# A hybrid convolution and linear-attention layer on eight cores: the context tile shares its first FFN's weight blocks with the fourth token tile, first loads in another order, one stream order for all sequences

## The chip, the cores and the metric

The kernel runs on all eight cores of one Trainium2 chip. The batch of 32 sequences is split over the cores, four to a core; the cores exchange nothing. The metric is the device time of the slowest core, in microseconds. The kernel before took 7987.3 us (median of three runs, 7969.67 to 7999.19).

## The reference, cut to what matters

```
x: (32, 2048, 1024) tokens    ctx: (32, 256, 1024) context tokens    D_FF = 2816
mx = split(silu(c) @ w_mod + b_mod, 9)          # shift, scale, gate for ffn1, mixer, ffn2
mc = split(silu(c_ctx) @ w_mod + b_mod, 9)      # the same map, for context tokens
half_ffn(h, ...): u = rmsnorm(h) * (1 + scale) + shift
                  a, b = split(u @ w_gu); h + 0.5 * gate * ((silu(a) * b) @ w_down)
x = half_ffn(x, ..., w1_gu, w1_down);  h = half_ffn(ctx, ..., w1_gu, w1_down)
# one input projection: conv input | q | k | v | output gate | decays | merge gates
# of the context only k, v and the decays are used: they give the start state of both scans
o = forward scan + backward scan (chunked gated linear attention, 4 heads)
y_conv = silu(layernorm(depthwise_conv31(glu(conv_in)))) @ w_conv_out
y_gla  = (rmsnorm(o) * silu(og)) @ w_gla_out
x = x + gate * ((sigmoid(ga) * y_conv + sigmoid(gb) * y_gla) @ w_out)
x = half_ffn(x, ..., w2_gu, w2_down);  out = rmsnorm(x) * g_final
```

## The kernel before

Activations lie with channels on partitions: a token tile is 8 x 128 channels by 512 tokens, and a sequence has four of them (i = 0 to 3) and a context tile of 256 tokens (i = 4). `JOBS` lists, for each sequence s, five "A" jobs (first FFN of tiles 0 to 3, then of the context) and four "D" jobs (second FFN of tiles 0, 3, 1, 2). `GID` numbers them; g is that number, nine to a sequence.

The program is made of streams, each a Python generator that yields groups of instructions. A scheduler (`Sched.run`) merges them into one fixed order for each engine: it holds a modelled time for each engine, each tile and the DMA, takes first a group without matmuls that could start within 1.5 us of TensorE's modelled time, else the first stream in order of priority whose matmul group is ready, else the group that is ready soonest. Streams wait for flags that other streams set; a flag only orders the instructions, while the semaphores that the program waits on come from the tiles that an instruction reads and writes. Each engine works through its own list in order; SP issues most DMAs, and GpSimd (POOL) issues the casting ones (fp32 to bf16) among its additions and powers.

The streams that matter here:

- `mod_stream` (priority 9): 36 half-chunks of w_mod, 1 MB each, into two buffers `WM` (in the trace wm_82 and wm_83); the first eight give shift and scale of the first FFN (flag ("mod", 1)), the others are spread over the FFN steps by `MOD_AT`.
- `n_stream` (8): `n1(job)` loads x in 128-token pieces into xtok, transposes it on TensorE into `X[g % 2]`, normalises and modulates it into `uF[g % 2]`; `n2(job)`, after the FFN, stores X (2 MB, x1_s) for a token tile and modulates into `U2[i]` for the mixer. n1 of the next tile goes before n2 of the present one.
- `f_stream` (3, raised to 5 for the first D job of sequence 0): for each job 22 up-projection steps (one 512 KB block `wgu`, 16 matmuls, silu on ACT, product on DVE) into hF, then 8 down-projection steps (one 704 KB block `wdn`, 22 matmuls). Flags ("fs", 30 g + step) mark the steps. Jobs 0 and 1 of sequence 0 already share their up-projection blocks (`pair`, second hidden tile hF2). `WL` fetches blocks ahead: where a weight is used for the first time it is cast by a POOL DMA and written back to a bf16 copy in HBM by SP, later it is loaded from that copy by SP.
- `pc_stream`, `pz_stream`, `pq_stream`, gate and state streams: the mixing stage. The convolution's projections start with tiles 0 and 1; q, k, v with tile 0 of head 0; both scans start from the context tile.
- `mp_stream`, `mh_stream`, `m_stream` (4.5, 4.6, 4): LayerNorm and head norms of each tile, then the merge, whose result feeds the D job of the tile. X alternates between two buffers, so the merge of one tile waits for the output of the D job two before its own (flag ("p", g - 2)).
- `c_stream` (1): in sequence 0 it casts 70 weights (48 of 256 KB in bf16, two buffers, and 22 of 512 KB, one buffer) for later stages, one for each mark; its marks are ("fs", 88) to ("fs", 149) and eight convolution steps. `setup` holds the first loads.

The lines the trace names: L638 is the DMA helper, L649 the matmul helper, L653 transposes, L665 ACT, L674 tensor_tensor, L677 scalar_tensor_tensor.

## Time and profile before

| | us |
|---|---|
| median of three runs | 7987.3 |
| the profiled execution | 7996.9 |
| its span on the slowest core | 7995.3 |
| TensorE busy in it | 7500.6 |
| VectorE, ScalarE, GpSimd busy | 2871.8, 2794.9, 1378.8 |

The page divides the span into 40 slices of some 200 us. TensorE's digit is 6 in the first slice, 9 in nearly all others, with 7 and 8 in some. All numbers of rows come from core 1, the slowest one. A matmul's recorded duration runs to the end of its pipeline, so a row's mean is longer than the step from one matmul to the next. In sequence 0 the first FFN runs from about 95 to 737 us, the mixing to about 1258, merge and second FFN to 2213; sequence 1 has its context stage from 2695 to 2766 us.

### The profile page before, as it was taken

The numbers are of one execution on the slowest core, as the hardware profiler recorded it, in microseconds if no ns is written. First come the engines' busy times: TensorE is split into PE (matmuls) and PEld (weight loads), VectorE is DVE, ScalarE is ACT, GpSimd is POOL, SyncE is SP. The second block draws the span as 40 slices with busy tenths as digits, with TensorE's granted clock in tenths as the row PEclk, the third lists the DMA queues.
The fourth block names the chain that finished last, engine by engine and source line by source line (L and its number), as shares of the span: only waits on it lengthen the run. The fifth ranks groups of instructions, "written<-read, shape, count | busy, mean of one in ns | idle before, by whom it ended". The sixth has DMA issues, their size and how long they took to land.

```text
span 7995.3 us, 125533 instructions; the slowest of 8 cores (7951.7 to 7995.3 us)
## 1 busy us (share of the span) xinstructions
PE 7500.6 (94%) x43682; PEld 3886.1 (49%) x43682; DVE 2871.8 (36%) x4652; ACT 2794.9 (35%) x5010; POOL 1378.8 (17%) x1138
## 2 busy tenths in 40 slices
PE   6997989789999999899999999999999999989999
PEld 3444544344444555444444464544444455544444
DVE  1221555222232256433232234633322324653322
ACT  2222664222222266422122245632222325653221
POOL 0111114222001100422101000141211011033210
PEclk8999999899999999999999998999999999999999
DMA  7888775364555524545555543554555562354544
GB/s 193 232 259 211 170 180 152 127 186 160 166 182 184 181 79 119 158 153 168 164 179 183 184 128 86 135 165 165 172 160 170 186 200 85 93 167 148 176 160 143
DMA packets 489205, 1300.37 MB, mean 163 GB/s; under 512 B 56464, under 2 KB 156048, under 8 KB 477840
## 3 DMA queue, kind: packets, MB, share of 16 engines
q1 hardware_dynamic: 468720, 1236.57, 49.1%
q0 software_dynamic: 19872, 55.78, 4.6%
q8 instruction: 367, 6.01, 0.3%
q14 instruction: 246, 2.02, 0.1%
HBM read 1166.36 MB, written 181.53 MB: 169 GB/s over the span
## 4 chain that ended last, share of the span: by engine, by line
PE 80%; DMA 10%; issue 3%; ACT 2%; DVE 2%; POOL 1%; SPq 1%; DVEq 0%; ACTq 0%; POOLq 0%
PE pb L649 78%; PE pb L653 2%; SPq L638 1%; DMA xtok_85<-x 1%; DMA L0rz_135<-z_s 1%; DMA wgu_96<-gu_s 1%; DMA wdn_101<-dn_s 1%; DMA wgu_95<-gu_s 0%; DMA L1rz_193<-z_s 0%; DMA wf_s<-w2k_80 0%; DMA w2k_80<-w_in_f 0%; POOL mac_118 L674 0%; DMA wgu_97<-gu_s 0%; DMA xtok_84<-x 0%; DMA w2k_81<-wf_s 0%
## 5 line engine op out<-in xcount | busy, mean ns | idle before, releaser
L674 DVE TENSOR_TENSOR hF<-ft_102,pb 128x512 bf16<-128x512 f32 (+1 forms) x396 | 260.2, 657 | 855.6 <-PE pb L649 739.8
L674 DVE TENSOR_TENSOR hF<-ft_103,pb 128x512 bf16<-128x512 f32 (+1 forms) x374 | 244.9, 655 | 748.4 <-PE pb L649 684.8
L665 ACT ACTIVATE ft_103<-pb 128x512 f32<-128x512 f32 (+1 forms) x396 | 225.6, 570 | 736.1 <-PE pb L649 732.2
L665 ACT ACTIVATE ft_102<-pb 128x512 f32<-128x512 f32 (+1 forms) x396 | 225.5, 569 | 730.0 <-PE pb L649 725.3
L649 PE MATMUL pb<-hF,wdn_100 128*128 128x512 bf16 (+1 forms) x2068 | 448.8, 373 | 15.8 <-DMA wdn_100<-dn_s 11.5
L649 PE MATMUL pb<-hF,wdn_101 128*128 128x512 bf16 (+1 forms) x2046 | 432.2, 367 | 10.7 <-DMA wdn_101<-dn_s 7.1
L649 PE MATMUL pb<-hF,wdn_99 128*128 128x512 bf16 (+1 forms) x2046 | 430.9, 366 | 11.7 <-DMA wdn_99<-dn_s 6.4
L649 PE MATMUL pb<-uF_88,wgu_97 128*128 128x512 bf16 (+1 forms) x1712 | 378.7, 374 | 25.3 <-ACT ft_102 L665 18.0
L649 PE MATMUL pb<-uF_89,wgu_95 128*128 128x512 bf16 (+1 forms) x1728 | 378.7, 371 | 8.8 <-ACT ft_102 L665 5.9
L677 DVE SCALAR_TENSOR_TENSOR X_86<-pb,SC,X_86 128x512 f32<-128x512 f32 (+1 forms) x208 | 151.9, 730 | 638.2 <-PE pb L649 633.1
L649 PE MATMUL pb<-uF_89,wgu_96 128*128 128x512 bf16 (+1 forms) x1728 | 374.6, 368 | 5.1 <-DMA wgu_96<-gu_s 5.1
L649 PE MATMUL pb<-uF_88,wgu_98 128*128 128x512 bf16 (+1 forms) x1712 | 372.1, 369 | 1.5 <-DMA wgu_98<-gu_s 1.4
L677 DVE SCALAR_TENSOR_TENSOR X_87<-pb,SC,X_87 128x512 f32<-128x512 f32 (+1 forms) x208 | 151.9, 730 | 609.6 <-PE pb L649 609.4
L649 PE MATMUL pb<-uF_89,wgu_98 128*128 128x512 bf16 (+1 forms) x1440 | 317.7, 373 | 13.3 <-ACT ft_103 L665 11.8
L649 PE MATMUL pb<-uF_88,wgu_96 128*128 128x512 bf16 (+1 forms) x1456 | 319.1, 370 | 11.8 <-ACT ft_103 L665 5.9
L649 PE MATMUL pb<-uF_88,wgu_95 128*128 128x512 bf16 (+1 forms) x1456 | 318.0, 370 | 10.3 <-DMA wgu_95<-gu_s 10.3
L649 PE MATMUL pb<-uF_89,wgu_97 128*128 128x512 bf16 (+1 forms) x1440 | 315.5, 370 | 10.5 <-DMA wgu_97<-gu_s 10.5
L649 PEld LDWEIGHTS pb<-hF,wdn_100 128*128 128x128 bf16 x2068 | 202.8, 98 | 247.7 <-issue 28.0
L649 PEld LDWEIGHTS pb<-hF,wdn_99 128*128 128x128 bf16 x2046 | 200.1, 98 | 228.5 <-issue 17.0
L649 PEld LDWEIGHTS pb<-hF,wdn_101 128*128 128x128 bf16 x2046 | 200.6, 98 | 226.8 <-issue 15.7
L649 PEld LDWEIGHTS pb<-uF_88,wgu_97 128*128 128x128 bf16 x1712 | 169.9, 100 | 210.8 <-issue 39.1
L649 PEld LDWEIGHTS pb<-uF_89,wgu_95 128*128 128x128 bf16 x1728 | 170.0, 99 | 194.5 <-issue 19.2
(730 smaller groups left out, 13378.0 us busy)
## 6 DMA issues: line engine op xcount, KB each, us to landing
wgu_97<-gu_s SPq DMA_DIRECT2D x187, 512.0 KB, 4.0
wgu_98<-gu_s SPq DMA_DIRECT2D x187, 512.0 KB, 4.1
wgu_95<-gu_s SPq DMA_DIRECT2D x187, 512.0 KB, 4.1
wgu_96<-gu_s SPq DMA_DIRECT2D x187, 512.0 KB, 4.1
wdn_101<-dn_s SPq DMA_DIRECT2D x91, 704.0 KB, 4.7
wdn_99<-dn_s SPq DMA_DIRECT2D x91, 704.0 KB, 4.6
wdn_100<-dn_s SPq DMA_DIRECT2D x90, 704.0 KB, 4.7
w2k_78<-wf_s SPq DMA_DIRECT2D x166, 256.0 KB, 3.1
```

The lines of the kernel that those rows point to most:

```text
L638: S.op(q, lambda e: e.dma_start(out=out, in_=in_, **kw), reads, writes, float(nb), dma=True)
L649: S.op("pe", lambda e: e.matmul(out, lhsT, rhs, start=start, stop=stop), reads, writes, c)
L653: S.op("pe", lambda e: e.transpose(out, in_, idn), reads, writes, c)
L665: S.op("act", lambda e: e.activation(out, in_, func, **kw), reads, writes, c)
L674: S.op(eng, lambda e: e.tensor_tensor(out, in0, in1, op), reads, writes, vcost(eng, fsz(out), fast))
L677: S.op("dve", lambda e: e.scalar_tensor_tensor(out=out, in0=in0, scalar=scalar, in1=in1, op0=op0, op1=op1), reads, writes, vcost("dve", fs ...
```

## The change

The context's first FFN no longer has steps of its own. In tile 3's job each weight block is used first for the context (256 columns), then for tile 3 (512 columns), in the up- and in the down-projection. For that the context has its own X (`Xc`, in the bytes of the merge buffers MTM), modulated input (`uFc`, in MRB) and hidden tile (`hF2c`, in the bytes of U2_3 and half of U2_4); its n1 follows n1 of tile 3, both before n2 of tile 2, and its n2 follows n2 of tile 3. Flags of both jobs are set at the end of the shared steps.

The first loads: wal, dwp, rmask, smask and gfin move from `setup` to `setup_later`, after step 4; w_mod has three buffers for its first eight half-chunks; the first weight blocks are asked for after half-chunk 5 (flag "mw"); tile 0 does its first three steps alone before tile 1 is waited for.

The order: the raised priority of `f_stream` in sequence 0 is gone; the blocks of all jobs of a sequence are listed at once; `c_stream` may issue two casts for each step of tile 3's job and one at each of the first eight convolution steps. `pc_stream` asks for its first blocks at step 8 of tile 3's job.

```diff
+              sb("wm2", [128, 4, 512], F32, Area([(loc_lo[0], loc_lo[1])]))]
+        hF2c, t_hF2c = sb("hF2c", [128, NJ, 256], BF16, Area([(loc_lo[3], loc_lo[3] + 12288)]), parts=NJ)
+        Xc = sb("Xc", [128, 8, 256], F32, Area([span_of(rts(MTM))]), parts=8)
+        uFc = sb("uFc", [128, 8, 256], BF16, Area([span_of(rts(MRB))]), parts=8)
...
+        def setup_later():
+            dma("sp", wal[:], wal_d, writes=[t_wal], nb=256 * 1024)
...
+            dma("sp", gfin[:], gfin_d[0:1, :].to_broadcast((128, D)), writes=[t_gfin], nb=512 * 1024)
...
+            wbuf = lambda cc: WM[cc % 3 if cc < 8 else cc % 2]
...
+                S.flag(("mw", cc))
...
+                if cc + 3 < 8:
+                    fetch(cc + 3)
...
+        def XB(job):
+            return Xc if job[1] == "A" and job[2] == 4 else X[GID[job] % 2]
...
-                if nxt < len(JOBS) and JOBS[nxt][1] == "A":
+                if nxt < len(JOBS) and JOBS[nxt][1] == "A" and JOBS[nxt][2] < 4:
...
                     yield from n1(JOBS[nxt])
+                    if JOBS[nxt][2] == 3:
+                        yield from n1(JOBS[nxt + 1])
...
-                    if s == 0:
-                        S.prio("f", 5)
...
+                if kind == "A" and i == 4:
+                    continue
...
+                if g == 0:
+                    yield ("wait", ("mw", 5))
...
+                two = kind == "A" and i == 3
+                jobs = [JOBS[1], job] if g == 0 else [JOBS[g + 1], job] if two else [job]
+                if g == 1:
+                    steps = []
+                elif g == 0:
+                    steps = [(0, [1]), (1, [1]), (2, [1]), (0, [0]), (1, [0]), (2, [0])] + [(j, [0, 1]) for j in range(3, NJ)]
+                else:
+                    steps = [(j, list(range(len(jobs)))) for j in range(NJ)]
...
+                for k, (j, which) in enumerate(steps):
...
+                    for x in which:
+                        jb = jobs[x]
+                        if g == 0 and k in (3, 6):
+                            yield ("wait", ("u", 1))
+                        if two and j == 0:
+                            yield ("wait", ("u", g + 1))
...
+                    for jb in (jobs if two else [job]):
+                        Xb, tX = XB(jb)
...
                 S.flag(("f", g))
-                if s == 0 and kind == "D" and i == 0:
-                    S.prio("f", 3)
+                if two:
+                    S.flag(("fs", 30 * (g + 1) + 29))
+                    S.flag(("f", g + 1))
...
-                b = LB[GID[(s, "A", 4)] % 2]
+                b = LB[GID[(s, "A", 3)] % 2]
...
-                yield ("wait", ("u", g))
+                yield ("wait", ("fs", 30 * (g - 1) + 8))
...
-            marks = [("fs", 88 + k) for k in range(62)] + [("cv", 0, c, i) for c in range(2) for i in range(4)]
+            fs = [("fs", 88), ("fs", 89)] + [("fs", 90 + k // 2) for k in range(60)]
+            marks = fs + [("cv", 0, c, 0) for c in range(8)]
+            yield ("wait", ("fs", 4))
+            setup_later()
```

## Rows read from the trace of the kernel before

**Rows 1.** The page's busy time of each engine (share, count)

```profile
PE 7500.6 (94%) x43682; PEld 3886.1 (49%) x43682; DVE 2871.8 (36%) x4652; ACT 2794.9 (35%) x5010; POOL 1378.8 (17%) x1138
```

**Rows 2.** By stretch: length, engines' busy us (count), clock, DMA share, GB/s

```profile
0.00:103.10 103.10, 38.29 (x362) 28.95 (x363) 18.39 (x36) 27.83 (x48) 5.69 (x12) 0.75 0.72 190
510.50:640.40 129.90, 122.04 (x565) 56.40 (x564) 31.31 (x50) 30.75 (x54) 22.53 (x31) 0.97 0.93 247
640.40:737.00 96.60, 68.50 (x546) 55.52 (x545) 19.13 (x39) 17.80 (x39) 14.15 (x22) 0.89 0.92 254
2577.50:2695.30 117.80, 117.80 (x565) 55.85 (x564) 31.49 (x50) 30.64 (x54) 10.56 (x9) 1.00 0.58 188
2695.30:2766.50 71.20, 63.18 (x545) 54.09 (x544) 18.98 (x39) 17.82 (x39) 6.63 (x8) 0.95 0.73 245
```

**Rows 3.** The same, sum over context stages of sequences 1, 2, 3

```profile
sum 215.20, PE 189.26 PEld 161.87 DVE 56.94 ACT 53.49 POOL 19.88; mean PE 63.09 PEld 53.96 DVE 18.98 ACT 17.83 POOL 6.63
```

**Rows 4.** Matmuls of sequence 1's context stage: busy us, mean ns, idle

```profile
L649 PE MATMUL pb<-hF,wdn_99 128*128 128x256 bf16 x66 | 7.7, 272 | 1.8 <-DMA wdn_99<-dn_s 1.6
```

**Rows 5.** TensorE's waits in that stage: us in total, times, longest

```profile
PE pb L649 <- DMA wgu_97<-gu_s: 4.5, 1, 4.5
```

**Rows 6.** DMA issues in that stage: count, KB each, median us to landing

```profile
x_s<-X_86 SPq DMA_DIRECT2D x1, 2048.0 KB, 11.1
```

**Rows 7.** Busy by stretch: merge and second FFN, sequences 0 and 1; a part

```profile
1375.00:2213.20 838.20, 763.38 (x3609) 372.40 (x3610) 237.26 (x346) 196.17 (x324) 169.20 (x135) 0.95 0.51 159
3363.40:4129.70 766.30, 746.30 (x3599) 361.84 (x3598) 236.37 (x346) 194.89 (x323) 162.93 (x127) 0.98 0.51 166
1530.00:1630.00 100.00, 46.96 (x184) 30.89 (x183) 32.68 (x47) 26.87 (x43) 35.89 (x28) 0.65 0.27 74
```

**Rows 8.** TensorE's waits in the first of these: us, times, longest

```profile
PE pb L649 <- POOL mac_117 L674: 22.0, 1, 22.0
```

**Rows 9.** Tile and context U: ns min/median/max, first and last start

```profile
L665 ACT ACTIVATE U_3_67<-ntm_109,SC x4: 712/722/722, 2706.7 to 2711.8; 128x512 bf16<-128x512 f32 x4
...
L649 PE MATMUL pb<-U_4_68,wq_70 x16: 272/273/283, 2804.5 to 2831.8; 128*128 128x256 bf16 x16
L665 ACT ACTIVATE U_4_68<-ntm_109,SC x4: 492/501/508, 2780.3 to 2788.5; 128x256 bf16<-128x256 f32 x4
```

**Rows 10.** DMA from 2 to 28 us: queues' share of 16 engines; an issue

```profile
q0 software_dynamic: 720, 2.43, 66.2%
q1 hardware_dynamic: 1268, 2.31, 32.4%
...
xtok_84<-x SPq DMA_DIRECT2D x1, 512.0 KB, 23.1
```

**Rows 11.** DMA from 32.3 to 73 us: the same two

```profile
q1 hardware_dynamic: 1558, 9.86, 75.1%
...
xtok_84<-x SPq DMA_DIRECT2D x1, 512.0 KB, 8.0
```

**Rows 12.** Timeline of the start: start us, duration us, instruction

```profile
32.33 0.42 SPq L638 DMA_DIRECT2D wm_82<-w_mod  x1
...
75.84 0.23 DVE L677 SCALAR_TENSOR_TENSOR SC<-modT,vecs 128x40 f32<-128x40 f32 x1
...
95.43 3.62 PE L649 MATMUL pb<-uF_88,wgu_95 128*128 128x512 bf16 x16
```

**Rows 13.** Casts of sequence 0, first and last of 33; bytes of that stretch

```profile
515.31 0.57 POOL L638 DMA_DIRECT2D w2k_80<-w_in_f  x1 [1.56 <-DMA wf_s<-w2k_80]
...
736.41 0.57 POOL L638 DMA_DIRECT2D w2k_80<-w_conv_out  x1
...
DMA packets 18855, 56.65 MB, mean 250 GB/s; under 512 B 2096, under 2 KB 2096, under 8 KB 18455
```

**Rows 14.** Cold w2_down in sequence 0: ns, first and last start

```profile
L649 PE MATMUL pb<-hF,wdn_100 x43: 379/379/631, 1630.1 to 1649.8; 128*128 128x512 bf16 x43
L638 POOL DMA_DIRECT2D wdn_100<-w_down x2: 532/586/639, 1605.7 to 1636.7; - x2
```

More of the change, by code:

```diff
@@ L770, in mod_stream @@
                 if cc == 0:
-                    fetch(0)
-                    fetch(1)
+                    for k in range(3):
+                        fetch(k)
                 elif MOD_AT[cc] > 0:
@@ L851, in modulate, with UB @@
                 yield
+        def XB(job):
+            return Xc if job[1] == "A" and job[2] == 4 else X[GID[job] % 2]
+        def UB(job):
+            return uFc if job[1] == "A" and job[2] == 4 else uF[GID[job] % 2]
         t_x1 = [T(f"x1_{i}") for i in range(NTT)]
@@ L919, in n2 @@
             W, col = jw(job), jcol(job)
-            Xb, tX = X[g % 2]
+            Xb, tX = XB(job)
             acc, t_acc = accF[g % 2]
@@ L972, in n_stream @@
                     yield from n1(job)
-                if job[1] == "D" and job[2] == 0:
-                    pass
-                if nxt < len(JOBS) and JOBS[nxt][1] == "A":
+                if nxt < len(JOBS) and JOBS[nxt][1] == "A" and JOBS[nxt][2] < 4:
                     if g >= 1:
@@ L1013, in f_stream @@
                 yield ("wait", ("u", g))
-                Xb, tX = X[g % 2]
-                u, tu = uF[g % 2]
-                gn = 2 if kind == "A" else 8
-                acc, t_acc = accF[g % 2]
-                sides = [(u, tu, hF, t_hF)]
-                if pair:
-                    yield ("wait", ("u", 1))
-                    sides.append((uF[1][0], uF[1][1], hF2, t_hF2))
-                hb_, t_hb = (hF2, t_hF2) if g == 1 else (hF, t_hF)
-                for j in (() if g == 1 else range(NJ)):
-                    wb, t_wb = wl_g.get(ng)
-                    ng += 1
-                    S.flag(("fs", 30 * g + j))
-                    for (uu, tuu, hh_, t_hh) in sides:
+                two = kind == "A" and i == 3
[6 more added lines that the diff above has]
+                    steps = [(j, list(range(len(jobs)))) for j in range(NJ)]
+                hid = {job: (hF2, t_hF2) if g == 1 else (hF, t_hF)}
+                if len(jobs) == 2:
+                    hid[jobs[0]] = (hF2, t_hF2) if g == 0 else (hF2c, t_hF2c)
+                wj = {}
+                for k, (j, which) in enumerate(steps):
+                    if j not in wj:
+                        if g == 0 and j < 3:
+                            wl_g.ahead = 3 - j
+                        wj[j] = wl_g.get(ng)
+                        wl_g.ahead = 3
+                        ng += 1
+                        S.flag(("fs", 30 * g + j))
+                    wb, t_wb = wj[j]
+                    for x in which:
[4 more added lines that the diff above has]
+                            yield ("wait", ("u", g + 1))
+                        uu, tuu = UB(jb)
+                        hh_, t_hh = hid[jb]
+                        W = jw(jb)
                         pa, t_pa = FB.next()
@@ L1040, in f_stream @@
                         yield
-                if s == 0 and kind == "A" and i == 0:
+                if g == 0:
                     yield ("wait", ("mod", 2))
+                gn = 2 if kind == "A" else 8
                 for o in range(8):
@@ L1055, in f_stream @@
-                    yield
-                    if o == 0:
-                        act(acc[:, :W], Xb[:, o, :W], AF.Square, [tX[o]], [t_acc])
+                    for jb in (jobs if two else [job]):
+                        Xb, tX = XB(jb)
+                        acc, t_acc = accF[GID[jb] % 2]
+                        W, col = jw(jb), jcol(jb)
+                        hb_, t_hb = hid[jb]
+                        pd, t_pd = FB.next()
+                        for j in range(11):
+                            mm(pd[:, :W], wb[:, j, :], hb_[:, j, :W], j == 0, False, [t_wb, t_hb[j]], [t_pd])
@@ L1058, in f_stream @@
                         yield
-                    else:
-                        sq, t_sq = FQ.next()
-                        act(sq[:, :W], Xb[:, o, :W], AF.Square, [tX[o]], [t_sq])
+                        for j in range(11, NJ):
+                            mm(pd[:, :W], wb[:, j, :], hb_[:, j, :W], False, j == NJ - 1, [t_wb, t_hb[j]], [t_pd])
                         yield
-                        tt(acc[:, :W], acc[:, :W], sq[:, :W], ALU.add, [t_acc, t_sq], [t_acc], eng="pool")
+                        stt(Xb[:, o, :W], pd[:, :W], SC[:, col, gn, o:o + 1], Xb[:, o, :W], ALU.mult, ALU.add, [t_pd, t_SC[gn], tX[o]], [tX[o]])
@@ L1064, in f_stream @@
                         yield
+                        if o == 0:
+                            act(acc[:, :W], Xb[:, o, :W], AF.Square, [tX[o]], [t_acc])
+                            yield
+                        else:
+                            sq, t_sq = FQ.next()
+                            act(sq[:, :W], Xb[:, o, :W], AF.Square, [tX[o]], [t_sq])
+                            yield
+                            tt(acc[:, :W], acc[:, :W], sq[:, :W], ALU.add, [t_acc, t_sq], [t_acc], eng="pool")
+                            yield
```

69 lines of the change are left out of this document (28 added, 41 removed).

## The prediction

> **What bounds the kernel now.** I began with the busy shares: TensorE is busy for 94% of the span [rows 1], so only the stretches where it is not can give anything. Then I cut the span at the stage borders and read each stretch against one that does the same work undisturbed [rows 2]. An FFN tile of 512 tokens in sequence 1 takes 117.8 us with TensorE busy for all of it: there is nothing to gain there. The context tile that follows takes 71.2 us, and in sequences 1 to 3 together it takes 215.2 us [rows 3]. Its matmuls have 256 columns. One group of 66 is busy 7.7 us with 272 ns for one [rows 4]; it is three runs of 22, so one run is 2.57 us = 21 steps + 0.27, a step of 0.109 us. Its 22 x 16 + 8 x 22 = 528 matmuls need 57.6 us, plus some 1.9 us for the 17 others in the stretch (545 in all [rows 2]): 59.5 us, 178.5 for three. What is above that, 36.7 us, goes with the wait for weights: the longest one is for wgu_97 [rows 5], and beside it stands the 2 MB store of the tile before, 11.1 us to landing [rows 6]. Half the columns use up the same weight bytes in half the time. In sequence 0 the same two stages take 129.9 + 96.6 = 226.5 us against 117.8 + 59.5 = 177.3.
>
> Two more stretches stand out. The first 103.1 us have 38.3 us of matmul [rows 2]. And the merge with the second FFN of sequence 0 takes 838.2 us, where sequence 1 takes 766.3 for the same work [rows 7]: 71.9 us more. In it lies a stretch of 100 us with TensorE busy 47.0 at a granted clock of 0.65 [rows 7]; the longest wait there is 22.0 us for a GpSimd addition of the LayerNorm [rows 8]. In the other sequences the up-projection fills these gaps; here it ran before them, in one piece, under its raised priority.
>
> **The change part by part.** The terms are made against the profiled execution, 7996.9 us (span 7995.3 and 1.6 around it), which is 0.12% above the median of the three runs, 7987.3.
>
> Context tile with token tile 3, sequences 1 to 3. Each block of 16 matmuls a side is now used for 16 x 0.109 + 16 x 0.22 = 5.3 us (0.22 is 117.8 us by 528) where the context stage used it for 1.7, and the reload of 22 x 512 and 8 x 704 KB, 16.9 MB, goes in each sequence. The loads of a 512-column tile are hidden at 3.5 us a block [rows 2], so they are at 5.3. I take 1 us a sequence as left: +33.7. What is moved: the context's n1 goes into tile 2's FFN, where ACT and DVE are busy 31 us of 118 [rows 2], cost 0. The normalisations n2 of tile 3 and of the context now both come after the FFN, with the 2 MB store in front of them on SP's queue, and the first mixing loads behind it. Before, tile 3's last U step began 16.5 us after its FFN's end (2711.8 against 2695.3), and the context's eight took from about 2779 to 2789 and were first read at 2804.5, 38 us after the FFN's end at 2766.5 [rows 9]. In a row the two end after some 17 + 10 = 27 us, before the 38, so they are covered by the projections of tiles 0 to 2; if that cover were gone it would be 10 us a sequence. The store costs between 0 and its 11.1 us [rows 6] a sequence, because the convolution's own store and reload chain queues behind it; I take 3, nearer to 0 as the projections of tiles 0 to 2 need no new block at once. Term: 33.7 - 9 = **+25**, bounds +1 and +37.
>
> First loads. Before, x is asked for with the four casting weight loads of GpSimd and the broadcast of gfin in flight, and lands after 23.1 us [rows 10]; the first w_mod load waits in SP's order behind the reuse of that buffer and goes out at 32.33 [rows 12]. After the change only scT, vecs and cst are ahead of x, and the casts follow GpSimd's first pow, so x should land after about 8 us (this is what xtok took among the w_mod loads [rows 11]) and the first w_mod load go out at about 13: 19 us earlier. From there the modulation is ready 43.5 us later (32.33 to 75.84 [rows 12]). The casts now fall into that stretch: they took 66.2% of the engines for 26 us, 17 us of work [rows 10], while w_mod took 75.1% of 40.7 us, 30.6 us [rows 11]. The sum is 48 us at full use; the third buffer lets the gaps be used, so I take 50 us, 7 more than now. The modulation is ready 12 us earlier. Beside that, three column steps of tile 0 come before tile 1 is needed, where one did before (3.62 us [rows 12]): 7 us. Term: **+19**, bounds 0 (casts wholly in the way, 19 - 17, and the fillers hidden anyway) and +39 (no cast in the way).
> What the rows show of sharing is q0 at 66.2% and q1 at 32.4% while both had work [rows 10]. The Trainium skill (DMA: Bandwidth & Descriptors, Queues, rings and completion order) says that each engine goes round robin between queues, packet by packet. The trace agrees only in that both move; by an even turn x would have landed sooner in the kernel before, and the sum would lose some 5 us of the 19.
>
> Sequence 0, tile 3 with context. The excess there is 226.5 - 177.3 = 49.2 us. The conversion stream (fp32 to bf16 weights for later stages, a cast on GpSimd and a write-back on SP, two buffers) issued 33 casts from 515.31 to 736.41 [rows 13], 6.7 us each. Now two may be issued per block; the order on SP is fixed, so a write-back that waits for its cast holds the weight loads behind it. With 33 casts in the paired stage and 30% fewer bytes (16.9 of 56.65 MB [rows 13]) I expect about 5.3 us each, 175 us, so TensorE's 177 would bound; with 44 casts 233 us would. I take 211 us: **+15**, bounds -20 and +45. What is not cast there is cast in the mixing stage, so little is given back later.
> By the Trainium skill (DMA: Bandwidth & Descriptors, Anatomy of one DMA) a load costs about 2 us and its bytes at 436 GB/s; a cast and its write-back would take about 6 us for each buffer, 3 us for each of two, and this term would be +45. The rows show more than twice that for a cast, so I hold to them.
>
> One order in sequence 0. The second FFN loses its raised priority, so its up-projection no longer runs in one piece (before the norm and head work of the next tile) but fills that work's gaps, as in sequence 1. This takes away the 71.9 us, but not the cold w2_down: its first cast is issued at 1605.70 and the first matmul on it runs at 1630.1 [rows 14], 24.4 us. In the new order the next merge waits for that tile's output, so nothing covers these. Term: 71.9 - 24.4 = **+47**, bounds 0 and 72.
>
> Sum: 25 + 19 + 15 + 47 = 106 us. 7996.9 - 106 = 7891; scaled by 7987.3 / 7996.9 it is **7881 us**.
>
> **The rivals.** (a) The conversion stream throttles the paired stage. At 6.7 us for each of 60 casts it would last 402 us, 175 more than 226.5: 25 + 19 - 175 + 47 = -84, a time of 8071, slower than before. It decides from about 47 casts in that stage (47 x 6.7 = 315, which eats the other 91 us). For it: casts waited for write-backs in every step before. Against: only 33 went out where 60 were allowed, so the buffers set the pace and not the marks. (b) The order of sequence 0 gives nothing because the cold w2_down is put off until all else is done, as before: 47 of the gain are lost, 7928. (c) The mixing stages start later: store and two n2 exposed for 10 us in all four sequences, 40 of the gain are lost, 7921. The 11 us between 27 and 38 speak against it. (d) All goes well: casts out of the way (20 more), conversions hidden (30 more), the order worth all 72 (25 more): a gain of 181 instead of 106, 7806. (e) The edit does less than it says, the context's matmuls being bound by something other than weights (weight loading into the array, say): then 34 of the gain are lost, 7915; the 0.109 us step in rows that wait for nothing speaks against it.
>
> **How the numbers follow.** Forecast 0.58 (own range 7835 to 7925), (a) 0.05, (b) 0.13, (c) 0.10, (d) 0.10, (e) 0.04. The range reaches half-way to (d) and beyond (b), (c) and (e) by the forecast's own 20 us: 7810 to 7945. A measurement of this kernel can tell about 0.5%, 40 us, from no change: faster means under 7947, slower over 8027. The forecast and (d) are faster, most of (b), (c) and (e) too (0.20 of 0.27), with 0.07 in between; (a) is slower for 0.04 and in between for 0.01. So 0.88, 0.08, 0.04.
>
> **What would show it.** Right: paired stages of 175 to 180 us in sequences 1 to 3 (now 117.8 + 71.2 = 189) with no wait for wgu; the first w_mod load before 16 us and the first FFN matmul before 70; in sequence 0 a paired stage between 180 and 230 us; its merge stage at 780 to 800 us with no 22 us wait for mac_117. Wrong: a first read of the context's U later after the FFN's end than the 38 us of now, w_mod loads behind casts, or a paired stage in sequence 0 in which each block takes two cast round trips.

## The result, and the profile after

The changed kernel takes 7890 us (7887.1 and 7892.7), the kernel before 7987.3 at the median: a ratio of 0.988, 95% interval 0.9836 to 0.9925. That is some 97 us less, more than the 40 us that can be told from no change. The forecast was 7881, its range 7810 to 7945. Cores of a die whose granted clock lay under 0.96 are left out of all times in this document.

The time is that of the slowest core, and this is not the same core in the two profiles (core 1 before, core 6 after; within one run the cores lie up to 51 us apart). So I cut every core's trace at the same marks and took the mean over the eight cores, whose spans fell from 7974.7 to 7862.0 us, by 112.7. The marks: F, the last w1_down matmul of tile 2's FFN; E, the last one of the FFN of tile 3 and context; M, the first merge matmul on MT; N, the first product hF of the next sequence, or the end. In us, before, after and gained:

| stretch | sequence 0 | sequence 1 | sequence 2 | sequence 3 |
|---|---|---|---|---|
| start (or N) to F: tiles 0 to 2 | 508.3, 500.2: **8.1** | 361.8, 365.3: -3.5 | 361.5, 364.7: -3.2 | 362.0, 365.8: -3.8 |
| F to E: tile 3 and context | 230.9, 181.6: **49.3** | 188.7, 173.3: 15.4 | 189.3, 173.3: 16.0 | 189.8, 173.3: 16.5 |
| E to M: mixing | 604.0, 626.6: **-22.6** | 566.0, 573.9: -7.9 | 572.2, 574.9: -2.7 | 565.6, 575.9: -10.3 |
| M to N: merge and second FFN | 874.0, 808.6: **65.4** | 797.6, 798.6: -1.0 | 797.2, 800.2: -3.0 | 806.0, 805.8: 0.2 |

By the prediction's terms: first loads **8** (19 were forecast); sequence 0's tile 3 with context 49, of which 23 are given back in the mixing behind it, **27** (15); one order in sequence 0 **65** (47); tile 3 with context in sequences 1 to 3 47.9 - 10.5 - 20.9 - 3.8 = **13** (25). They add up to 113 where 106 stood: two terms that came out too small (by 23 us) stood against two that came out too large (by 30), so it is partly luck that the total was this near.

The same stretches on the page's core, by windows (length, engines' busy us and count, clock, DMA share, GB/s): the start, tile 3 with context in sequence 0, tile 2's FFN of sequence 1, tile 3 with context there, and sequence 0 from M to N.

```profile
0.00:72.00 72.00, 30.87 (x314) 22.71 (x316) 10.27 (x24) 16.86 (x29) 4.05 (x10) 0.71 0.78 213
497.74:678.09 180.35, 175.05 (x1056) 106.12 (x1073) 39.81 (x69) 35.37 (x69) 34.66 (x52) 0.99 0.84 207
2376.00:2499.16 123.16, 122.33 (x593) 60.47 (x604) 39.47 (x63) 42.59 (x75) 11.56 (x10) 1.00 0.58 192
2499.16:2672.62 173.46, 172.51 (x1056) 105.29 (x1073) 39.77 (x69) 35.38 (x69) 14.98 (x15) 1.00 0.32 110
1323.80:2135.10 811.30, 775.57 (x3681) 378.45 (x3754) 250.09 (x366) 206.77 (x343) 182.24 (x147) 0.98 0.54 167
```

The paired FFN of sequence 1 is TensorE from end to end at the full clock; its DMA share is 0.32, where the two stages had 0.58 and 0.73 [rows 2], and TensorE's waits in it show none for weights. All eight cores take 173.3 us for it in each of the three sequences. In sequence 0 it has 7 us more. The busy shares hardly move [rows 1], since what was removed was mostly idle time. The page's core lacks 733 of TensorE's 43682 records; on core 5, where none is missing before or after, TensorE's busy time fell by 25 us (7491.1 to 7466.1) and the span by 118 (7987.1 to 7868.7). The page:

```profile
PE 7426.2 (94%) x42949; PEld 3872.2 (49%) x43682; DVE 2885.0 (37%) x4652; ACT 2796.4 (35%) x5014; POOL 1379.5 (17%) x1138
```

TensorE's longest waits from 1388 to 2135 us (us in total, times, longest), for [rows 8]: the 22 us for mac_117 are gone, and the cold w2_down shows as 4.1 us.

```profile
PE pb L653 <- ACT ft_104 L669: 11.9, 2, 5.9
PE pb L653 <- DMA w2k_81<-wf_s: 6.7, 2, 6.3
PE pb L653 <- DMA wdn_102<-w_down: 2.7, 1, 2.7
...
PE pb L653 <- DMA wdn_103<-w_down: 0.8, 1, 0.8
PE pb L653 <- DMA wdn_101<-w_down: 0.6, 1, 0.6
```

Two places where time came back. The context's U in sequence 1 (ns min/median/max, first and last start; FFN's end at 2672.6), for [rows 9]: the last writes of tile 3's U start 24 us after the FFN's end, those of the context's 42, and its first read is at 2717.3, 45 us behind. Each tile's rows stand under its own view.

```profile
L669 ACT ACTIVATE U_3_67<-ntm_110,SC x4: 706/712/722, 2685.9 to 2695.6; 128x512 bf16<-128x512 f32 x4
L669 ACT ACTIVATE U_3_67<-ntm_111,SC x4: 705/710/721, 2686.5 to 2696.7; 128x512 bf16<-128x512 f32 x4
```

```profile
L653 PE MATMUL pb<-U_4_68,wq_70 x16: 272/273/283, 2717.3 to 2745.9; 128*128 128x256 bf16 x16
...
L669 ACT ACTIVATE U_4_68<-ntm_111,SC x4: 492/508/508, 2706.0 to 2714.6; 128x256 bf16<-128x256 f32 x4
```

And sequence 0 behind its paired FFN (timeline of TensorE: start, length, instruction, idle before it and its releaser). The broadcasts of the two norms (out of stn_58 and stn_59) stand in TensorE's queue ahead of the first head projection on U_0. U_0 was ready long before; the projection's weight wq_69 was asked for at 681.74 us and took 6.5 us to land, so about 7 of the 10 us of waiting fall after both were there:

```profile
681.94 1.02 PE L653 MATMUL pb<-ones_45,accF_109 128*128 128x1 f32 x8 [0.40 <-POOL accF_109 L678]
685.09 1.73 PE L653 MATMUL pb<-cst,stn_58 128*128 128x128 f32 x8 [2.12 <-POOL stn_58 L678]
686.61 0.85 PE L653 MATMUL pb<-ones_45,accF_108 128*128 128x1 f32 x4
695.37 1.19 PE L653 MATMUL pb<-cst,stn_59 128*128 128x128 f32 x4 [7.91 <-POOL stn_59 L678]
```

### The profile page after: what moved, and what is told of

It reads as the page before. It is cut to its first block, busy times and chain, and to the rows that moved or that the text cites. A ratio compares the mean times of both kernels' runs of the same rounds, so it can differ in the third digit from the quotient of the medians.

```text
span 7891.2 us, 124318 instructions; the slowest of 8 cores (7840.0 to 7891.2 us)
## 1 busy us (share of the span) xinstructions
PE 7426.2 (94%) x42949; PEld 3872.2 (49%) x43682; DVE 2885.0 (37%) x4652; ACT 2796.4 (35%) x5014; POOL 1379.5 (17%) x1138
## 4 chain that ended last, share of the span: by engine, by line
PE 79%; DMA 11%; issue 3%; ACT 2%; DVE 2%; SPq 1%; POOL 1%; another core or an unknown queue 0%; DVEq 0%; ACTq 0%; POOLq 0%
PE pb L653 78%; PE pb L657 2%; SPq L642 1%; DMA w2k_81<-w_in_f 1%; DMA stage<-w_gu 1%; DMA xtok_86<-x 1%; DMA gu_s<-stage 1%; DMA wf_s<-w2k_81 1%; DMA w2k_80<-sq_s 1%; DMA w2k_81<-w_gla_out 0%; DMA L1rz_196<-z_s 0%; DMA L1rz_197<-z_s 0%; DMA L0rz_139<-z_s 0%; DMA z_s<-L1zt_193 0%; DMA wm_83<-w_mod 0%
## 5 line engine op out<-in xcount | busy, mean ns | idle before, releaser
L678 DVE TENSOR_TENSOR hF<-ft_105,pb 128x512 bf16<-128x512 f32 x394 | 270.7, 687 | 869.2 <-PE pb L653 788.1
L669 ACT ACTIVATE ft_105<-pb 128x512 f32<-128x512 f32 x396 | 234.9, 593 | 703.8 <-PE pb L653 696.7
L669 ACT ACTIVATE ft_104<-pb 128x512 f32<-128x512 f32 (+1 forms) x396 | 216.1, 546 | 710.9 <-PE pb L653 706.1
L678 DVE TENSOR_TENSOR hF<-ft_104,pb 128x512 bf16<-128x512 f32 x288 | 197.9, 687 | 607.5 <-PE pb L653 502.1
L653 PE MATMUL pb<-hF,wdn_102 128*128 128x512 bf16 x1784 | 408.0, 381 | 11.3 <-DMA wdn_102<-w_down 4.5
L653 PE MATMUL pb<-hF,wdn_101 128*128 128x512 bf16 x1785 | 407.9, 381 | 9.8 <-DMA wdn_101<-w_down 4.0
L653 PE MATMUL pb<-hF,wdn_103 128*128 128x512 bf16 x1764 | 402.0, 380 | 6.5 <-DMA wdn_103<-dn_s 2.5
L681 DVE SCALAR_TENSOR_TENSOR X_87<-pb,SC,X_87 128x512 f32<-128x512 f32 x192 | 144.2, 751 | 584.8 <-PE pb L653 584.6
L681 DVE SCALAR_TENSOR_TENSOR X_88<-pb,SC,X_88 128x512 f32<-128x512 f32 x192 | 144.2, 751 | 577.1 <-PE pb L653 577.1
L653 PE MATMUL pb<-uF_89,wgu_97 128*128 128x512 bf16 x1386 | 325.5, 383 | 12.5 <-ACT ft_104 L669 5.9
L653 PE MATMUL pb<-uF_90,wgu_99 128*128 128x512 bf16 x1378 | 323.1, 384 | 13.8 <-ACT ft_104 L669 12.2
L653 PE MATMUL pb<-uF_90,wgu_100 128*128 128x512 bf16 x1365 | 320.2, 384 | 14.2 <-ACT ft_105 L669 11.9
L653 PE MATMUL pb<-uF_89,wgu_99 128*128 128x512 bf16 x1356 | 319.2, 385 | 13.7 <-ACT ft_104 L669 11.8
L653 PE MATMUL pb<-uF_90,wgu_97 128*128 128x512 bf16 x1377 | 322.4, 383 | 6.5 <-ACT uF_90 L669 4.6
L653 PE MATMUL pb<-uF_89,wgu_98 128*128 128x512 bf16 x1394 | 323.1, 380 | 2.0 <-issue 0.7
L653 PE MATMUL pb<-uF_89,wgu_100 128*128 128x512 bf16 x1351 | 314.6, 381 | 8.4 <-ACT ft_105 L669 5.9
L653 PE MATMUL pb<-uF_90,wgu_98 128*128 128x512 bf16 x1373 | 318.2, 380 | 2.1 <-issue 0.3
L653 PEld LDWEIGHTS pb<-hF,wdn_102 128*128 128x128 bf16 x1826 | 179.0, 98 | 224.8 <-issue 14.9
L653 PEld LDWEIGHTS pb<-hF,wdn_101 128*128 128x128 bf16 x1826 | 179.2, 98 | 223.8 <-issue 13.8
L653 PEld LDWEIGHTS pb<-hF,wdn_103 128*128 128x128 bf16 x1804 | 176.5, 98 | 216.1 <-issue 8.2
L653 PEld LDWEIGHTS pb<-uF_89,wgu_97 128*128 128x128 bf16 x1424 | 140.1, 99 | 173.5 <-issue 18.5
L653 PEld LDWEIGHTS pb<-uF_90,wgu_99 128*128 128x128 bf16 x1408 | 138.9, 99 | 175.2 <-issue 21.6
```

What stands on the lines that cost most here:

```text
L653: S.op("pe", lambda e: e.matmul(out, lhsT, rhs, start=start, stop=stop), reads, writes, c)
L669: S.op("act", lambda e: e.activation(out, in_, func, **kw), reads, writes, c)
L678: S.op(eng, lambda e: e.tensor_tensor(out, in0, in1, op), reads, writes, vcost(eng, fsz(out), fast))
L681: S.op("dve", lambda e: e.scalar_tensor_tensor(out=out, in0=in0, scalar=scalar, in1=in1, op0=op0, op1=op1), reads, writes, vcost("dve", fs ...
```

## Experiments

Spans and stage times are means over cores, with the number of dies or cores in brackets. The mean span of a die is 7976 us for the kernel before (30 dies) and 7858 for the changed one (5). Dies of one kernel scatter with a standard deviation of 2 to 20 us, so effects under 10 us are read from the stages alone. These scatter too: in the runs that leave a stage of sequence 0 as it is in the changed kernel (e1, e4, e6, e7, e12, as far as each does), F to E takes 180 to 186 us and E to N 1433 to 1439; E to M of the later sequences takes 574 to 584 where no edit touches it. GLA stands for the gated linear attention, a gate matmul is one on wal.

### The order in sequence 0

e1: the raised priority put back into the changed kernel.

```diff
                 if kind == "D" and i == 0:
                     yield ("wait", ("bdone", s))
+                    if s == 0:
+                        S.prio("f", 5)
...
                 S.flag(("f", g))
+                if s == 0 and kind == "D" and i == 0:
+                    S.prio("f", 3)
```

> The changed kernel with the raised priority of the first second-FFN tile in sequence 0 put back (the order part of the change undone, all else kept). Theory: the order is worth about 65 us, because of the 72 us of rows 7 only about 11 us of cold w2_down remain. Then this kernel takes 65 us more than the changed one (about 7955), all of it in the merge and second FFN of sequence 0, where one stretch of about 85 us of up-projection runs in one piece and the GpSimd wait of about 22 us returns. The prediction's term says 47 us (7937). Rival (b) says nothing (7890).

Measured: M to N of sequence 0 takes 872.4 us instead of 808.6, **63.8** more, and no other stretch moves by more than the scatter; the mean span is 7938 (6 dies), 80 more, of which 64 lie in this stage. The 22 us are back (TensorE's waits, core 2, 1343 to 2170 us):

```profile
PE pb L653 <- POOL mac L678: 23.7, 2, 22.0
```

e2: the same priority taken out of the kernel before, and nothing else.

> The kernel before with only the raised priority taken out (the order part of the change alone). Theory: 65 us less than before (about 7922), sequences 1 to 3 and the startup unchanged to 2 us. The prediction's term says 47 us less (7940). If the order needs another part of the change to pay, less than that; rival (b) says no change (7987).

Measured: 7903 us (2 dies) against 7976, **73** less. There are no stage times for this run. Within the scatter the order alone gives as much as it does inside the change: it needs none of the other parts.

### The start

e6: no column steps of tile 0 ahead of tile 1.

```diff
-                    steps = [(0, [1]), (1, [1]), (2, [1]), (0, [0]), (1, [0]), (2, [0])] + [(j, [0, 1]) for j in range(3, NJ)]
+                    steps = [(j, [1, 0]) for j in range(NJ)]
...
-                        if g == 0 and k in (3, 6):
+                        if g == 0 and k == 0 and x == 0:
                             yield ("wait", ("u", 1))
```

> The changed kernel without the three column steps of tile 0 that run before tile 1 is needed: the first up-projection step waits for both tiles. The prediction gave these steps 7 us. Theory from the trace of the changed kernel: they ran at the lower clock and tile 1's matmuls waited until 91 us anyway, so they bring the end of this up-projection forward by only 4 us (251.5 us now, about 255 then; 258.5 by the prediction), and TensorE's first matmul of this FFN comes at about 85 instead of 65.7. What is left at the start of tile 3 is the same 4 us.

Measured: the up-projection of tiles 0 and 1 ends at 257.3 instead of 251.5 us, F comes at 508.1 instead of 500.2: 6 to 8 us, nearer to the prediction's 7 than to the 4 expected here (the granted clock on the changed kernel's core 6 was 0.82 from 65 to 91 us, a mix of its two levels, so not all of these steps ran at the lower one). The mean span is 7873 (5 dies). TensorE's first FFN matmul stays at 66.9 us and not at 85: in this edit tile 0's share of the first step still runs ahead while tile 1 is waited for, as in the kernel before, so two steps are undone and not three.

e7: the tables and gfin ahead of x, casts at once; third buffer and column steps kept.

```diff
             act(scT[:], scT[:], AF.Silu, [t_scT], [t_scT])
+            setup_later()
...
-                if g == 0:
-                    yield ("wait", ("mw", 5))
...
-            yield ("wait", ("fs", 4))
-            setup_later()
-            yield
```

> The changed kernel with the first loads in the order of before: the four small tables and the broadcast of gfin ahead of x, and GpSimd's first weight casts issued at once; third w_mod buffer and column steps stay. The prediction gave the order of the loads 12 us. Theory: the modulation is ready 10 us later (about 74 instead of 63.7), and 10 us of that is still there at the end of the up-projection (about 261) and at the end of the program. Rival: the modulation is later, but the casts that are done earlier give it back, so that the end of the up-projection moves by less than 4 us.

Measured: the modulation is ready at 70.2 us (63.7 in the changed kernel, 73.8 before), the up-projection ends 8.6 us later, F comes 4.6 us later. So the order of the loads is worth 6.5 us at the modulation, and the other 3.6 are left for the third buffer, which no run takes out alone. Of the 8.6 us 4.0 are lost again by F: the down-projection of tiles 0 and 1 takes 102.8 us in the changed kernel, 99.1 here and 99.8 before. Why stays open; it is not the moved loads themselves, which go out at 106 to 114 us on the page's core, over 130 us ahead of that stage. Neither theory had this half. The mean span is 7871 (5 dies).

### Tile 3 with context in sequence 0

e8: no conversion before this FFN has ended.

```diff
-            marks = fs + [("cv", 0, c, 0) for c in range(8)]
+            marks = [("f", 4)] * len(small + large)
```

> The changed kernel with the whole conversion stream (70 items) held back until the paired FFN of sequence 0 has ended; nothing is left out. Now this stage takes 201 us there and 171 in sequences 1 to 3. Theory: these 30 us are the weight loads that stand behind write-backs on SP's queue; without them the stage takes 172 to 180. By the prediction (what is not cast there is cast in the mixing stage and little is given back) the program would be about 20 us faster. Rival: the mixing stage of sequence 0, which has some 30 casts of its own until 362 us, cannot take 40 more: 70 casts at 9 to 11 us end at 630 to 770 us where the merge's first weights are due at 605, so this stage grows by 20 to 150 us and the program is slower.

Measured: F to E takes 173.3 us on all cores, as in the other sequences (181.6 with conversions), and E to M 760.8 instead of 626.6: **134 us longer**, 7984 in all (4 dies). The window of that FFN on core 1:

```profile
514.68:688.14 173.46, 173.46 (x1074) 105.29 (x1073) 39.72 (x69) 35.38 (x69) 16.63 (x18) 1.00 0.31 103
```

In the paired FFN the conversions cost 8.3 us (7 to 13 by the runs that leave it as it is) and not the 30 that I had read: my 201 and 171 us ran to the first head projection and held the wait for the norms shown above. The rival holds: on core 1 the last cast is issued 626 us behind the first head projection, and the merge of sequence 0 waits for the end of the conversions. Its load of OG stands on SP's queue behind the last four write-backs, and TensorE waits 29.5 us for what is made of it (timeline of SP, then of TensorE):

```profile
1311.98 25.62 SPq L642 DMA_DIRECT2D gu_s<-stage  x4
1337.69 1.71 SPq L642 DMA_DIRECT2D OG<-o_s  x3
...
1346.23 1.84 PE L653 MATMUL pb<-ones,mtm 128*128 128x1 f32 x8 [29.47 <-POOL mtm L678]
```

e10: 14 casts moved from the mixing into tile 2's FFN, through one buffer.

```diff
-            marks = fs + [("cv", 0, c, 0) for c in range(8)]
...
+            marks = [("fs", 60 + 2 * k) for k in range(14)] + fs
...
+                if n == 14:
+                    yield ("wait", "mod_done")
...
```

> The changed kernel with 14 of the 70 conversions moved from the mixing stage of sequence 0 into tile 2's FFN, one for every two weight blocks, through one buffer; nothing is left out. In the mixing stage of sequence 0 the last convolution comes at 518 us (475 in the other sequences) and the merge's first matmul 87 us behind it, as in the kernel before (510 and 87); there the GLA's end at 501 would allow 594. Theory: the rest of the conversion stream holds the convolution's stores and reloads on SP's queue; with 14 casts fewer the last convolution comes some 20 us earlier, the merge's first matmul at 590 to 597 instead of 605, and tile 2's FFN grows by less than 10 us: between 0 and 15 us are gained in all. Rival: the casts cost tile 2's FFN what they cost the paired stage (30 us for 44 of them, 0.7 us each, 10 us), and the mixing stage stays: some 10 us slower.

Measured: slower, 7886 (7 dies). F comes 6.8 us later, the paired FFN takes 5.0 more, and E to N together 1445.8 us where the changed kernel takes 1435.2. (In e12, whose sequence 0 is that of the changed kernel, F comes 3.2 later and the paired FFN takes 4.4 more, so of the first two little is clear of the scatter; the third is.) The last convolution did not come earlier (525 us behind the first head projection, 518 before), so the number of casts left in the mixing is not what holds it. What does stays open; on the page's core TensorE's longest wait from 1200 to 1350 us is for one of its reloads (us in total, times, longest):

```profile
PE pb L653 <- DMA L1rz<-z_s: 13.9, 1, 13.9
```

### The mixing stages of sequences 1 to 3

e4: the 2 MB store behind both norms instead of ahead of them.

```diff
-            if i < 4:
+            if i < 3:
                 dma("sp", x1_s[i], Xb[:], reads=tX, writes=[t_x1[i]], nb=1 << 21)
...
+            if i == 4:
+                j3 = (s, "A", 3)
+                dma("sp", x1_s[3], XB(j3)[0][:], reads=XB(j3)[1], writes=[t_x1[3]], nb=1 << 21)
```

> The changed kernel with the 2 MB store of tile 3's result issued behind both LayerNorms instead of ahead of them; nothing is left out. The prediction put 3 us a sequence on this store (bounds 0 to 11.1). Theory: the store delays nothing, since the first projections need no new block; the mixing stages of sequences 1 to 3 stay within 1 to 2 us, or grow a little because the store now meets the convolution's own stores. Rival: the store holds the first weight loads of the mixing stage on SP's queue; then each of them is about 3 us shorter or more.

Measured (two cores): E to M 576.4, 572.0 and 574.3 us; the changed kernel has 573.9, 574.9 and 575.9. No cost of the store can be seen: the mean is 0.7 us less, well inside the scatter. The mean span is 7868 (4 dies).

e3: both norms started together (sums, rsqrt, broadcasts), then the two modulations. The new function n2_both is left out here.

```diff
...
-                yield from (n2(job) if job[1] == "A" else o_post(job))
+                if job[1] == "A" and job[2] == 3:
+                    yield from n2_both(job, JOBS[nxt])
+                else:
+                    yield from (n2(job) if job[1] == "A" else o_post(job))
```

> The changed kernel with the two LayerNorm chains behind the paired FFN (token tile 3 and context) started together: sums, rsqrt and broadcasts of both first, then the modulation of tile 3, then of the context; nothing is left out. In the changed kernel the context's U is ready 42 us after the FFN's end and first read at 45, where it was ready at 22 and read at 38 before. Theory: this serial chain delays the gates by 7 us and with them the end of each mixing stage in sequences 1 to 3. Then U of the context is ready at about 34 us, is read at about 38, and each of these three mixing stages is 6 to 8 us shorter (some 20 us in all). Rival: the mixing stages are longer by the 2 MB store in front of the first loads and by the TensorE work of the norm that moved into them; then the gates start earlier and the stages stay within 2 us.

Measured (four cores): the last writes of the context's U start 39 us behind the FFN's end instead of 42, not 34; the first gate matmul comes at 49.1, 46.3 and 49.1 us (50.8 in the changed kernel), E to M takes 580.3, 564.6 and 581.7. Inconclusive: 4.5 us earlier gave 10 in sequence 2, but 1.7 earlier gave nothing in 1 and 3, where a convolution had now slipped in ahead of the context's projection (31 us instead of 37). The mean span is 7871 (6 dies). In sequence 0 the wait for the second norm is gone with this edit: the first head projection comes 12.1 us behind E instead of 21.8, and TensorE's longest wait for a norm there is 1.7 us (core 6). Yet E to M takes 630.5 us (626.6) and E to N 1438.0 (1435.2): nothing is gained.

e5: in addition the context's modulation as one GpSimd product and eight VectorE operations.

```diff
...
+            tt(Xn[:], Xn[:], RBC[0][:, None, :].to_broadcast((128, 8, 256)), ALU.mult, tXn + [RBC[1]], tXn, eng="pool")
...
+                        ts(U2[4][0][:, c, :], Xn[:, c, :], SC[:, jcol(jc), 3, c:c + 1], SC[:, jcol(jc), 4, c:c + 1], ALU.mult, ALU.add,
...
```

> The changed kernel with the context's second LayerNorm taken off the serial chain: both sums, rsqrt and broadcasts together, the context's product with the rsqrt as one GpSimd multiplication, its scale and shift as eight VectorE operations; nothing is left out. In the run with both norms started together the modulations still ran one behind the other (10 us each on ACT and VectorE), so the context's U came 3 us earlier only (39 against 42 us after the FFN's end) and the three mixing stages were 645, 629 and 646 us, where the changed kernel has 638, 640 and 640. Theory (the gates' start sets the end of the stage): U of the context is ready at about 30 us and read at about 38, the first gate matmul comes at 44 where it is 51 now, and each mixing stage of sequences 1 to 3 is about 8 us shorter, 630 us. Rival (the stage's length goes by the order in which its streams are issued, not by the start of the gates): the gates start earlier, the stages stay at 640 with a scatter of 5 to 10 us and no common sign.

Measured: 7861 us (4 dies), no different from 7858. There are no stage times for this run: as a test of the gates it says nothing, as an edit it gains nothing.

e9: in addition to e5, the context's projection ahead of tile 3's and no convolution before it.

```diff
...
+                    yield ("wait", ("qk", s, 0, 4))
                     yield ("wait", ("rzl", s, c, i))
...
-                    for (i, t0, W) in (spans if h == 0 else spans[::-1]):
+                    for (i, t0, W) in ([spans[k] for k in (0, 1, 2, 4, 3)] if h == 0 else spans[::-1]):
```

> The kernel with the context's norm on GpSimd and VectorE (last call), and besides the first projection reads the context's U ahead of tile 3's and no convolution runs before that; nothing is left out. The gates begin with the context, in both directions. In all runs so far the last GLA output comes 426 to 440 us after the first gate matmul and the second FFN begins 156 to 160 us after that, whatever the gates' start was (44 to 51 us). Theory (the gates' start sets the end of the mixing stage in sequences 1 to 3): the first gate comes at 33 to 37 us instead of 51, each of the three stages takes about 625 us instead of 640, and the mean of the cores' spans falls from 7860 to about 7815. Rival (the order of issue decides): the gates start early, and the stages stay at 640, each 5 to 10 us to either side.

Measured: the first gate matmul comes at 39.3, 36.1 and 39.0 us and E to M takes 565.5, 564.4 and 565.9 us, 8.4, 10.5 and 10.0 less than in the changed kernel. Gate matmuls of sequence 2, the changed kernel (FFN's end 4582.2) and then e9 (4580.1), each with ns min/median/max and first and last start:

```profile
L653 PE MATMUL pb<-L1lr,wal x80: 374/587/692, 4632.9 to 5013.9; 17*128 17x512 f32 x64, 17*128 17x256 f32 x16
```

```profile
L654 PE MATMUL pb<-L1lr,wal x80: 374/587/852, 4616.1 to 4998.5; 17*128 17x512 f32 x64, 17*128 17x256 f32 x16
```

The gates start 15 us earlier, end 13 us earlier, and the stage ends 10 earlier. That is what the theory says. The edit changes the order of issue too, so the rival is not shut out by this run alone; but in sequences 1 to 3 of the kernel before, the changed one and e9 alike, the last GLA output comes 429 to 437 us behind the first gate matmul and M 92 to 94 us behind that output. There is one limit that the theory lacked: the last convolution now comes at 478 us and the last GLA output at 472, and M is 87 to 88 us behind the convolution, where sequence 0 of the changed kernel, in which the convolution comes last, has 86. So the two are about level, and by an estimate from these numbers still earlier gates would give 1 to 2 us more. In sequence 0 nothing is gained (E to N 1439.1 against 1435.2). The mean span is 7844 (5 dies).

e12: e9's edits in sequences 1 to 3 only.

> The edits of the run in which the context is projected first, in sequences 1 to 3 only; sequence 0 is that of the changed kernel; nothing is left out. Theory: in sequence 0 it is not the gates that end last but the convolution (its last matmul at 518 us, the merge 87 us behind it), so there the early context gained nothing and cost 14 us (683 against 669); in sequences 1 to 3 it gains 9 to 11 us each. Then the mixing stage of sequence 0 takes 669 us, the other three 630, and the mean of the cores' spans is 30 us below the changed kernel's, about 7830. Rival: the 14 us in sequence 0 come from the scatter of that stage (660 to 692 us from core to core in the changed kernel), so this kernel is at 7837 again.

Measured: 7836 us (8 dies) against 7975 for the kernel before (13 dies measured beside it) and 7858 for the changed one. By its slowest core it takes 7858.0 and 7864.7, where the changed kernel takes 7887.1 and 7892.7. E to M takes 566.1, 570.4 and 566.9 us in the later sequences and 628.6 in sequence 0 (643.4 in e9). Sequence 0 is back where it was, as expected; but from E to N it is 1438.1, and e9 was no worse there (1439.1): what e9 lost ahead of M it had back behind it. This version is some 20 us faster than the changed kernel and not told from e9. Spans and clocks of its profiled execution:

```profile
die 0 (median of its cores): 7838.0 us, clock 0.973
die 1 (median of its cores): 7852.6 us, clock 0.973
```

e11: the edits of e9 and e10 together.

> The edits of the two runs above in one kernel. By the sum of the two theories the mean of the cores' spans is 7800 to 7815; by the two rivals 7860 to 7870.

Measured: 7866 us (3 dies). The later sequences are as in e9 (E to M 564 to 568 us on four cores); sequence 0 pays for the earlier casts, and more than in e10 (E to N 1466.5 against 1445.8): one theory and one rival.

## Why the prediction was right, and where it was not

**Tile 3 with context, sequences 1 to 3: 13 for 25.** That the context was bound by weights was right: 173.3 us on every core, none of it waiting for a block (175 to 180 had been named). The gain of 15.9 us a sequence is more than the 11.2 taken, but 3.5 of it was only moved: the context's n1 now runs in tile 2's FFN, where I costed it at nothing by ACT and VectorE. The engine to look at was TensorE, which is full there (window above): the context's 16 transposes and its broadcast of four matmuls lengthen that stage (112 and 44 of these two kinds in sequence 1 on core 5, where there were 96 and 40). Net 12.4 a sequence. The step that failed is "17 + 10 = 27 us, before the 38". The two norms in a row took 42.5: each has its sum, rsqrt and broadcast ahead of it (13.3 us to tile 3's first write, 7.0 more for the context, for which I had counted none), and tile 3's 16 modulation operations took 11 us where [rows 9] showed 6. VectorE and ACT now serve the first projections at that time; that this is the reason was not tested. So the first read slipped from 38 to 45 us, a sign that the prediction had named for being wrong, the gates by 7 and the stage by 7.0 in the mean, where I had 3 for the store, for which e4 shows no cost. That the stage follows the gates is shown by e9 and by the constant distances given there; e3 alone could not show it.

**First loads: 8 for 19.** The steps themselves held: the first w_mod load goes out at 12.11 us (13 was forecast), the modulation is ready at 62.5 on the page's core (63; 10.1 earlier in the mean of the cores), the column steps gave 6 to 8 (7). At the end of the up-projection 14.0 us were gained. What failed is that I took them as final: 3.0 are lost in the down-projection of tiles 0 and 1, which got longer for a reason that stays open (e7), and the other 3 in tile 2's FFN, which has the context's n1 in sequence 0 as well.

```profile
12.11 0.42 SPq L642 DMA_DIRECT2D wm_82<-w_mod  x1
```

```profile
62.46 0.23 DVE L681 SCALAR_TENSOR_TENSOR SC<-modT,vecs 128x40 f32<-128x40 f32 x1
```

How the column steps lie (timeline of TensorE): tile 0's begin at 65.17 in pieces, each behind a piece of its modulation, and tile 1's first matmul still waits until 90.92, so the steps fill a time in which TensorE had little but tile 1's transposes.

```profile
65.17 0.58 PE L653 MATMUL pb<-uF_89,wgu_97 128*128 128x512 bf16 x1 [3.11 <-ACT uF_89 L669]
66.18 1.25 PE L653 MATMUL pb<-uF_89,wgu_97 128*128 128x512 bf16 x2 [0.42 <-ACT uF_89 L669]
...
75.95 3.62 PE L653 MATMUL pb<-uF_89,wgu_98 128*128 128x512 bf16 x16
...
90.92 0.38 PE L653 MATMUL pb<-uF_90,wgu_97 128*128 128x512 bf16 x1 [3.17 <-ACT uF_90 L669]
```

The loads around them, 12 to 60 us (queues' share of 16 engines), for [rows 11]: now the casts are among the w_mod loads, as reckoned.

```profile
q1 hardware_dynamic: 1659, 10.24, 64.6%
q0 software_dynamic: 720, 2.82, 34.9%
```

**Tile 3 with context, sequence 0: 27 for 15.** The pace of the casts was right: through the two buffers 35 went out between 502.1 and 672.7 us on the page's core, 5.0 us each (5.3 forecast for 33; the 6.7 that it started from should have been 6.9, as 33 casts have 32 gaps), and the bytes fell from 56.65 [rows 13] to 37.39 MB (what SP's queue moved by two fifths, 46.80 to 26.87). By that the stage is near TensorE's 177; I chose 211, more than half-way to the 233 of a case with 44 casts where the rows had 33, and that choice was the mistake: 180.4 us came out. (The +45 that I had put beside it from the Trainium skill, DMA: Bandwidth & Descriptors, Anatomy of one DMA, lies near the 49 measured, but not by its price: that was 3 us a cast, and the trace has 5.0.) "Little is given back later" failed too, by 23 us: the last convolution comes 540.2 us behind E instead of 517.6, and M 86 us behind it in both kernels. The first head projection comes 21.8 us behind E instead of 7.1 in the mean, and 10 of these are the two waits for a rsqrt shown above. But they are not shown to be the cost: in e3 and e9 the first head projection comes at 12.1 and 13.0 us, and E to N of sequence 0 is no shorter (1438.0 and 1439.1). Fewer casts in the mixing (e10) did not shorten it either. What holds the convolution there stays open.

The DMA of that FFN, 497.7 to 678.1 us (packets and bytes; queue, packets, MB, share of 16 engines), for [rows 13]:

```profile
DMA packets 14770, 37.39 MB, mean 207 GB/s; under 512 B 1648, under 2 KB 1648, under 8 KB 14500
## 3 DMA queue, kind: packets, MB, share of 16 engines
q1 hardware_dynamic: 9072, 26.87, 45.2%
q0 software_dynamic: 5684, 10.33, 38.3%
```

**One order in sequence 0: 65 for 47.** The mechanism was right, and e1 (64) and e2 (73) show it alone. The mis-sized step is the cold w2_down: 24.4 us were taken off for it, from the cast to the first matmul [rows 14]. In the new order M to N of sequence 0 is 10.0 us longer than that of sequence 1 (808.6 and 798.6), and TensorE's direct waits for the casts are 4.1 us: the merge of the next tile did not have to stand still for the whole latency. So 10 us were left where 24.4 had been put.

**The rivals.** (a) would need the conversions to throttle the paired FFN; they cost it 8.3 us. (b) is excluded by e1 and e2, (e) by the 173.3 us. (c) came true for 7 us instead of 10 in three sequences; in sequence 0 the mixing took 23 us more, for a cause that stays open. (d) is what the order and the paired FFN of sequence 0 came near to. The range was wider than its reason: its lower end, 7810, lies almost at (d) (7806) and not half-way to it (7843); the measured time lies inside either.

## What to carry over

A step that is moved takes its load on every engine with it: ask of the stage that receives it which engine is full there, and of a chain that is now serial how long it takes when its engines have other work, not when they were free. Where two ends of an estimate come from two counts of the same thing, take the count that the trace shows and not a value in between. A wait that is plain in a timeline need not be what the stage pays for: take it out and measure the stage. And a sum can be right by terms that cancel: only marks that cut both traces at the same places, averaged over the cores, tell that.

## What the runs showed that I had not expected

A four-matmul broadcast that waits for a rsqrt stops TensorE for 7.9 us although for some 7 of them the projection behind it has its input and its weight, since each engine works through its list in order (sequence 0); with that wait gone (e3) the stage is no shorter. The 16 modulation operations of tile 3's norm took 6 us beside an FFN [rows 9] and 11 us beside the first projections. A cast and its write-back went from one in 6.9 us [rows 13] to one in 5.0 when the weight loads beside them became fewer.
